# MLP units in features form: high and low parts of x side by side, 512 columns a product, in a fp32-by-parts transformer kernel

## The reference, cut to what matters

```
def squared_relu_mlp(hn, w_up, w_down):
    return jnp.square(jax.nn.relu(hn @ w_up)) @ w_down
...
hf = _rms_norm(x, norm_ffn_pre[l])
u = _dwconv_causal(hf @ w_up[l], ffn_dw[l]) + ffn_dw_b[l]      # 3 taps along the tokens
u_g, u_v = jnp.split(u, 2, axis=-1)
yff = (jax.nn.silu(u_g) * u_v) @ w_down[l]
```

## Time and profile before

| | |
|---|---|
| median of 3 runs | 1291.28 us (1290.41 to 1294.0) |
| profiled execution | 1293.13 us, of which the span of instructions is 1291.4 us |
| PE busy | 98% of the span, 9836 matmuls |
| DVE busy | 64%; ACT 52% |
| DMA | 210.89 MB, mean 163 GB/s |
| granted TensorE clock | 0.993 of full speed on average |
| MLP 0, first product to last up unit's ReLU | 229.8 to 399.3 us |
| MLP 1, the same | 528.9 to 698.3 us |
| FFN, first product to the end of the span | 1098.7 to 1291.4 us |

### The profile page before, as it was taken

One profiled execution on the slowest core, in us unless ns is written; L12 is line 12 of the kernel. 1 busy time (PEld: TensorE's weight loads), 2 busy tenths in 40 slices (PEclk: granted clock), 3 DMA queues, 4 the chain that ended last, 5 costly groups with the idle time before them and its releaser, 6 DMA issues.

```text
span 1291.4 us, 23651 instructions
## 1 busy us (share of the span) xinstructions
PE 1259.2 (98%) x9836; PEld 1181.3 (91%) x9836; DVE 832.1 (64%) x1136; ACT 667.3 (52%) x935; POOL 58.6 (5%) x101
## 2 busy tenths in 40 slices
PE   8999899999999999999999999999999998999998
PEld 7998898999998998899998999999999987999997
DVE  5984357655556565655555579998656566776665
ACT  5973646454445544544444554655454445655543
POOL 4001011000000000000000000010000010000000
PEclk9999999999999999999999999999999999999999
DMA  7660114656554644465655466344546533555551
GB/s 233 184 185 34 69 35 162 217 207 190 178 185 145 229 133 163 139 204 194 195 192 166 153 207 187 121 147 134 174 154 196 196 118 111 180 196 196 181 177 65
DMA packets 160345, 210.89 MB, mean 163 GB/s; under 512 B 5542, under 2 KB 143220, under 8 KB 160261
## 3 DMA queue, kind: packets, MB, share of 16 engines
q1 hardware_dynamic: 157315, 202.77, 48.7%
q0 software_dynamic: 1904, 6.85, 1.5%
q10 hardware_dynamic: 1042, 0.07, 0.1%
HBM read 208.62 MB, written 1.05 MB: 162 GB/s over the span
## 4 chain that ended last, share of the span: by engine, by line
PE 83%; DVE 8%; ACT 3%; issue 2%; DMA 2%; SPq 1%; POOL 0%; DVEq 0%; POOLq 0%; ACTq 0%
PE bank L365 25%; PE bank L368 25%; PE bank L369 25%; DVE wlo L301 2%; PE bank L1275 2%; PE bank L1255 2%; ACT whi L293 1%; DMA raw<-in_dn_w_in 1%; ACT common L611 1%; PE bank L1283 1%; SPq L3125 1%; PE bank L1811 1%; DVE common L2351 1%; PE bank L1938 1%; PE bank L1897 1%
## 5 line engine op out<-in xcount | busy, mean ns | idle before, releaser
L301 DVE TENSOR_TENSOR wlo<-raw,whi 128x2048 fp32r<-128x2048 f32 x190 | 434.8, 2291 | 239.5 <-ACT whi L293 239.3
L365 PE MATMUL bank<-xhi,whi 128*128 128x256 f32 x1808 | 519.8, 288 | 6.6 <-DVE xlo L688 6.2
L369 PE MATMUL bank<-xhi,wlo 128*128 128x256 f32 x1808 | 513.4, 284 | 0.0
L368 PE MATMUL bank<-xlo,whi 128*128 128x256 f32 x1808 | 513.3, 284 | 0.0
L293 ACT ACTIVATE whi<-raw 128x2048 fp32r<-128x2048 f32 x190 | 362.7, 1911 | 167.5 <-PE bank L365 108.4
L365 PEld LDWEIGHTS bank<-xhi,whi 128*128 128x128 f32 x1808 | 348.2, 193 | 12.0 <-issue 7.7
L368 PEld LDWEIGHTS bank<-xlo,whi 128*128 128x128 f32 x1808 | 348.3, 193 | 2.8 <-issue 1.2
L369 PEld LDWEIGHTS bank<-xhi,wlo 128*128 128x128 f32 x1808 | 348.2, 193 | 0.0
L365 PE MATMUL bank<-whi,hhi 128*128 128x512 f32 x392 | 153.4, 391 | 0.8 <-DVE hlo L2658 0.8
L368 PE MATMUL bank<-wlo,hhi 128*128 128x512 f32 x392 | 153.1, 391 | 0.0
L369 PE MATMUL bank<-whi,hlo 128*128 128x512 f32 x392 | 152.7, 389 | 0.0
(11 more groups left out here) (350 smaller groups left out, 1509.7 us busy)
## 6 DMA issues: line engine op xcount, KB each, us to landing
raw<-in_mlp_w_up SPq DMA_DIRECT2D x32, 1024.0 KB, 5.4
raw<-in_mlp_w_down SPq DMA_DIRECT2D x32, 1024.0 KB, 4.9
raw<-in_w_in SPq DMA_DIRECT2D x22, 1024.0 KB, 5.3
raw<-in_w_up SPq DMA_DIRECT2D x22, 1024.0 KB, 5.1
raw<-in_w_gate SPq DMA_DIRECT2D x16, 1024.0 KB, 5.5
raw<-in_dn_w_in SPq DMA_DIRECT2D x15, 1024.0 KB, 5.8
raw<-in_mb_w_in SPq DMA_DIRECT2D x12, 1024.0 KB, 5.1
raw<-in_w_down SPq DMA_DIRECT2D x11, 1024.0 KB, 4.9
```

The costliest lines, as they stand in the source:

```text
L301: nc.vector.tensor_tensor(wlo[:, s, :], raw[:, V % RAW, :], f32(whi[:, s, :]), ALU.subtract).then_inc(lo_ready, 1)
L365: ins = pe.matmul(o, shi, mhi, start=first, stop=False, skip_group_check=True)
L368: pe.matmul(o, shi, mlo, start=False, stop=False, skip_group_check=True)
L369: return pe.matmul(o, slo, mhi, start=False, stop=last, skip_group_check=True)
```

## The change

In the up units of the two MLPs and of the FFN, and nowhere else, `xhi` and `xlo` become two halves of one tensor `xparts`, and two matmuls per (f, k) take the place of three: the low weights against `xhi` (256 columns, into columns 0 to 255 of a bank) and the high weights against `xhi` and `xlo` side by side (512 columns, into the whole bank). f = 0 and f = 1 have a bank each. The two sums in a bank are then added: ACT copies columns 256 to 511 to SBUF (`copy_low`), DVE adds columns 0 to 255 to it (`add_low`) and gives the bank back. In the MLP, ReLU then works in place in SBUF. In the FFN, Identity and the taps read the sum from a new place `cin`, one for each half. In the first unit of a stage, the products of the low weights come first and wait only for `xhi`.

```
+        def wide_features(pe, U, uses, n=0, i=0, norm=None):
+            s = U % RING
+            pe.wait_ge(lo_ready, at_unit(U + 1, n, i))
+            wh, wl = wview(whi, s, KT), wview(wlo, s, KT)
+            def low_weights(f, k, start):
+                return pe.matmul(uses[f].ps[:, 0:T], wl[:, k, f * P:(f + 1) * P], xhi[:, k, :], start=start, stop=False,
+                                 skip_group_check=True)
+            def high_weights(f, k, stop):
+                return pe.matmul(wide_sums(uses[f]), wh[:, k, f * P:(f + 1) * P], xparts[:, :, k, :], start=False,
+                                 stop=stop, skip_group_check=True)
...
+                for f in range(2):
+                    if uses[f].n:
+                        pe.wait_ge(uses[f].freed, uses[f].at(i))
+                    for k in range(KT):
+                        ins = low_weights(f, k, k == 0)
+                        if f == 0 and k == 0:
+                            ins.then_inc(unit_begun, 1)
+                        ins = high_weights(f, k, k == KT - 1)
+                    ins.then_inc(uses[f].filled, 1)
+        def copy_low(act, dst, uses, copied, i=0, f=None):
+            for f in range(2) if f is None else [f]:
+                act.wait_ge(uses[f].filled, uses[f].at(i) + 1)
+                nc.scalar.activation(dst[:, f * T:(f + 1) * T], uses[f].ps[:, T:2 * T], ACT.Copy)\
+                    .then_inc(copied[f].sem, 1)
+        def add_low(dve, dst, uses, copied, i=0, f=None):
+            for f in range(2) if f is None else [f]:
+                part = dst[:, f * T:(f + 1) * T]
+                dve.wait_ge(copied[f].sem, copied[f].at(i))
+                nc.vector.tensor_tensor(part, uses[f].ps[:, 0:T], part, ALU.add).then_inc(uses[f].freed, 1)
...
             def act_a(act, U, p_, uses, hi_, re_, copied, n=0, i=0):
                 split_hi(act, U, n, i)
+                copy_low(act, hid_r[:, p_, :], uses, copied, i)
+                for use in uses:
+                    act.wait_ge(use.freed, use.at(i) + 1)
+                nc.scalar.activation(hid_r[:, p_, :], hid_r[:, p_, :], ACT.Relu).then_inc(re_.sem, 1)
...
             def act_half(act, b, half, i):
                 split_hi(act, b.us[half], b.n, i)
+                copy_low(act, src, b.uses[half], b.low[2 * half:2 * half + 2], i)
+                for use in b.uses[half]:
+                    act.wait_ge(use.freed, use.at(i) + 1)
...
             def dve_half(dve, b, half, i):
                 split_lo(dve, b.us[half], b.n, i)
+                add_low(dve, src, b.uses[half], b.low[2 * half:2 * half + 2], i)
                 dve.wait_ge(b.y1[half].sem, b.y1[half].at(i))
```

More of the change, by code:

```diff
@@ L169, in build @@
         wlo = sb("wlo", [P, RING, UNIT], F32R)
[L170 to L171 removed]
+        xparts = sb("xparts", [P, 2, KT, T], F32R)
+        xhi, xlo = xparts[:, 0], xparts[:, 1]
         hhi = sb("hhi", [P, 2, 2, T], F32R)
@@ L417, in gemm_features, with wide_sums @@
             ins.then_inc(use.filled, 1)
+        def wide_sums(use):
+            return use.ps[:, :].rearrange("p (x t) -> p x t", x=2)
+        def wide_features(pe, U, uses, n=0, i=0, norm=None):
[8 more added lines that the diff above has]
+                                 stop=stop, skip_group_check=True)
+            if norm:
+                for half in range(2):
+                    for q in (half, 2 + half):
+                        pe.wait_ge(norm.hi[q].sem, norm.hi[q].value)
+                    for f in range(2):
+                        if half == 0 and uses[f].n:
+                            pe.wait_ge(uses[f].freed, uses[f].n)
+                        for k in range(4 * half, 4 * half + 4):
+                            ins = low_weights(f, k, k == 0)
+                            if f == 0 and k == 0:
+                                ins.then_inc(unit_begun, 1)
+                    for q in (half, 2 + half):
+                        pe.wait_ge(norm.parts[q].freed, norm.parts[q].n + 1)
+                    for f in range(2):
+                        for k in range(4 * half, 4 * half + 4):
+                            ins = high_weights(f, k, k == KT - 1)
+                        if half:
+                            ins.then_inc(uses[f].filled, 1)
+            else:
+                for f in range(2):
+                    if uses[f].n:
+                        pe.wait_ge(uses[f].freed, uses[f].at(i))
+                    for k in range(KT):
+                        ins = low_weights(f, k, k == 0)
+                        if f == 0 and k == 0:
+                            ins.then_inc(unit_begun, 1)
+                        ins = high_weights(f, k, k == KT - 1)
+                    ins.then_inc(uses[f].filled, 1)
@@ L888, in mlp @@
             dl = [unit(rows(down, 256 * (NB - 2))), unit(rows(down, 256 * (NB - 1)))]
[L889 to L894, removed]
+            ua = [[G[2 * p_ + f].use() for f in range(2)] for p_ in range(2)]
@@ new lines, in mlp @@
+            hi_s, f_s, lo_s, re_s = (x.many(2) for x in (hid_sq, hid_f32, hid_lo, hid_relu))
+            cp_s = [low_sum.many(2) for p_ in range(2)]
+            ul = [[G[2 * p_ + f].loop(loop, 1)[0] for f in range(2)] for p_ in range(2)]
+            hi_l, f_l, lo_l, re_l = (x.loop(loop, 2) for x in (hid_sq, hid_f32, hid_lo, hid_relu))
+            low = low_sum.loop(loop, 4)
+            cp_l = [low[0:2], low[2:4]]
+            ut = [[G[2 * p_ + f].use() for f in range(2)] for p_ in range(2)]
@@ L2744, in conv_mlp @@
             prod = [common[:, 2048 + 512 * b_:2560 + 512 * b_] for b_ in range(2)]
+            cin = [common[:, 3072 + 512 * half:3584 + 512 * half] for half in range(2)]
             y1 = Signal(sem("ffn_first_tap"))
@@ L2815, in static_block @@
                 us = [unit(features(W, 256 * j)), unit(features(W, FF + 256 * j))]
-                marks = (y1.many(2), mid.many(2), sl.next(), pr.next(), hid_sq.next(), hid_lo.next())
-                uses = [G[2 * (j % 2) + k].use() for k in range(2)]
+                marks = (y1.many(2), mid.many(2), taps.many(2), low_sum.many(4), sl.next(), pr.next(), hid_sq.next(), hid_lo.next())
+                uses = [[G[2 * half + f].use() for f in range(2)] for half in range(2)]
                 b = Blk(j % 2, 2 * j, 0, us, marks, uses)
@@ L2905, in pe_block @@
                 for half in range(2):
-                    gemm_features(pe, b.us[half], b.uses[half], xhi, xlo, b.n, i, norm=None if half else norm)
+                    wide_features(pe, b.us[half], b.uses[half], b.n, i, norm=None if half else norm)
             def pe_f(pe):
```

112 lines of the change are left out of this document (55 added, 57 removed).

## The result

The changed kernel takes **1310.56 us** (median of 4 runs, 1309.7 to 1314.09), the kernel before 1292.64 us beside it (4 runs, 1290.41 to 1294.01): a ratio of 1.0147, 95% interval 1.0126 to 1.0167. It is slower, as predicted, but by 17.9 us and not 9.6, and 1310.56 lies outside the range of 1294 to 1309.

What follows compares the result with a forecast made beforehand. PE bounded all three stages before; changed, the DVE-ACT chain would bound the FFN. MLPs -6.9, FFN +14.5 and clock +2 gave +9.6 us: 1301 us against 1291.3, range 1294 to 1309.

Steps and rivals of the forecast that it cites:

- the ring: FFN: `add_low` behind `split_lo` closes a serial chain through DVE and ACT, 18.1 us a block against PE's 16.53.
- Rival A: FFN: PE stays the bound, since DVE's work fits by sum; -11.4 us, 1280 us; chance 0.08.
- Rival B: FFN: the DVE-ACT chain holds but is short, 17.0 to 17.3 us; 1289 to 1295 us; chance 0.11.
- Rival C: Up units: the fixed 13.3 ns per matmul is not saved, only the chain is left; 1308 us; chance 0.06.
- the parts of the ring: FFN block: first half 6.15 us, second half with block end 11.97 us.
- one fixed 13.3 ns goes: Up units: each (f, k) falls from 360 to 346.7 ns, a unit from 5.76 to 5.55 us; MLPs -6.8 us.
- the additions at the ends of the MLPs: MLP ends: copy and additions lengthen the last chain, +0.45 us at MLP 0 and +0.9 us at MLP 1.
- The 0.9 us at the end of MLP 1: End of MLP 1: copy 0.42 and additions 0.45 us more, passed on whole to the addition to `h`.
- The earlier starts of the three stages: First unit of each stage: PE starts on `xhi` without `xlo`, 0.7 us earlier each, -2.1 us in all.
- Terms of the FFN: FFN: 201.7 us against 187.1, +14.6, taken as +15.2; +14.5 after the 0.7 us earlier start.
- The first block: FFN: the first block takes 15.2 us, 5.97 + 9.2, with taps in place of a down unit's Silu and splits.
- The clock at the end: FFN end: after PE idles some 10 us, last products run at the lower clock level, +2 us (0 to 3.5).

Runs made afterwards that it cites:

- After: The changed kernel as made, measured and profiled against the kernel before; 1310.56 us, ratio 1.0147.
- Experiment 2: Changed kernel with the two MLPs put back to three matmuls per (f, k), the FFN left changed; 1313.88 us, ratio 1.0162.
- experiment 4: Changed kernel with DVE's two additions ahead of the split of the weights in the FFN; 1293.28 us, ratio 1.0008.
- 8: Changed kernel with one more 128x256 addition on DVE ahead of the additions of every FFN half but the last; 1318.4 us, ratio 1.0207.
- 9: The kernel of experiment 4 with one more 128x256 addition on DVE for every FFN half but the last; 1293.29 us, ratio 1.0018.
- experiment 10: The kernel of 7 with, for each f, the eight low-weight matmuls first and then the eight of 512 columns; 1285.07 us, ratio 0.9961.
- Experiment 3: Changed kernel with the high and low part of x for one k side by side in memory; 1309.88 us, ratio 1.0138.
- experiment 5: The kernel of Experiment 3 with operand and bank also written as one flat run of 512 columns; 1314.07 us, ratio 1.0157.
- 1: Changed kernel with the FFN put back to three matmuls per (f, k), the two MLPs left changed; 1289.48 us, ratio 0.9986.
- 6: The kernel of experiment 4 with unit 3's split behind the first unit's own ReLU, Square and `hlo` in each MLP; 1290.83 us, ratio 0.9995.
- 7: Changed kernel with the edits of experiment 4, experiment 5 and 6 together; 1290.17 us, ratio 0.9987.

## Why the prediction was right about the direction and wrong about the size

**Right: the ring.** The prediction said that `add_low` behind `split_lo` closes a chain through DVE and ACT that is longer than PE's work. After shows each sign of it: Identity released by `add_low`, 18.3 us a block, seven short waits of PE and one of 10.4 us. Experiment 2 puts the loss in the FFN, 4 removes it by the order alone, 8 and 9 show that an operation on the chain counts in one order and not in the other. Rival A (PE stays the bound) is out in after; experiments 4 and 10 made it true of the kernel, but not its 1280 us; the saving per matmul that it counts on came out smaller. Rival B (a ring of 17.0 to 17.3 us) is out. Rival C (13.3 ns not saved, 1308 us) came nearer to 1310.56 than the forecast of 1301, and about half of its premise holds, as the next step shows.

**Right: the parts of the ring.** The first half is 6.24 us (1267.38 to 1273.62) for 6.15, the second with the block's end 12.04 (to 1285.66) for 11.97. Together it is 18.28 for the 18.1 that the prediction went on with, 1.4 us over the eight blocks of the loop.

**The step that failed first: "one fixed 13.3 ns goes"** per (f, k), so an up unit of 5.55 us and MLPs of -6.8. Seven pairs in after take 305.82 to 308.29 = 2.47 us:

```profile
305.82 0.28 PE L431 MATMUL bank<-xparts,wlo 128*128 128x256 f32 x1
...
308.29 0.28 PE L431 MATMUL bank<-xparts,wlo 128*128 128x256 f32 x1
```

That is 353 ns and not 346.7: 7 ns go. The turn is 11.11 us, 0.11 less than in the earlier trace rows and not 0.23. The 120 and 227 ns of the earlier trace rows came from rows of one width each, and the prediction added them for a pair in which the widths alternate. 3.6 us are saved in the MLPs, 3.2 fewer than forecast. The Trainium skill (TensorE: Matmul & The Clock Gate, section Back-to-back issue gap) gives 2.5 ns per matmul for isolated ones; what was measured here, 7 ns, lies between this and 13.3. Experiments 3 and 5 rule out the two pieces and the pattern. In 10, eight wide ones in a row and eight narrow ones regain 4 of the 6 missing ns, so most belongs to alternating the widths. The other 2 are in the wide matmuls: in the group above, eight of them take 1.84 us (308.19 to 310.03), 230 ns each and not 227. Why either is so stays open.

**The step that was missing: the first unit of MLP 0.** The prediction priced the additions at the ends of the MLPs and held that in between "PE stays the bound". It had not looked at what stands ahead of the additions where a load comes late: the split that waits for it, 4.82 us already before the change. The 1.87 us wait above is followed by a lower clock (window, its length, PE, PEld, DVE, ACT, POOL, then the granted clock, DMA share, GB/s):

```profile
240.00:244.00 4.00, 2.13 (x8) 1.44 (x7) 2.34 (x3) 3.52 (x5) 0.00 (x0) 0.86 0.84 245
244.00:248.00 4.00, 4.00 (x15) 3.20 (x14) 3.20 (x5) 1.87 (x3) 0.00 (x0) 0.71 0.39 103
```

Products of 512 columns are 0.43 us apart there (243.50 to 243.92), the lower of the two levels. What the two windows lack to full speed is 0.14 x 4 + 0.29 x 4 = 1.7 us. With the wait it is 3.6 us of the profiled execution. Experiment 3's profile has a wait of 1.8 us at the same place and no lower clock, so the 1.7 us are not in every execution. Of the seven profiles with this wait (1.6 to 1.9 us: after and experiments 1, 3, 4, 5, 8 and 9), two have the lower clock behind it, after and experiment 5. That the additions' place behind the split makes the wait is borne out by experiments 6 and 7, where the split goes behind them and the longest such wait is 0.5 us.

Both together explain why the FFN starts only 0.6 us earlier (1098.08 against 1098.68 in the earlier trace rows) and not 7.6: 3.2 and 3.6 of the 7.0 us that are missing. The 0.9 us at the end of MLP 1 came as forecast: the last product starts at 696.32 and ReLU at 697.68, 1.36 us later, where it was 0.32 (697.41 to 697.73), and 0.11 of the difference is that the product is now the wider one. From ReLU to the addition to `h` it is 5.3 us in both. The earlier starts of the three stages, 0.7 us each in the forecast, came about as it said: PE's waits for `xlo` fall by 2.9 us (6.2 in the earlier trace rows, 3.3 in after), and the first products now wait 0.9 us in sum for something else.

**Terms of the FFN.** From the first product to ACT's release in the last tile it is 208.00 us (1098.08 to 1306.08) for 186.47: +21.5, where 14.6 to 15.2 and 2 for the clock were forecast.

```profile
1306.08 0.60 ACT L671 ACTIVATE common<-bank 128x512 f32<-128x512 f32 x1 [4.11 <-PE bank L371]
```

The 4.3 us more are several small ones. The first addition comes 6.66 us after the start and not 6.0 (+0.7): ACT had copied the bank at 1103.41, but DVE was in its splits up to 1104.74. The first block takes 16.64 us and not 15.2 (+1.4): its first half is 7.01 us instead of 5.97, and the split in it waits 1.04 us for `split_hi`, which waits for a load; the rest is 9.63 instead of 9.2, with an `ACT_TABLE_LOAD` of 1.28 us ahead of Silu for which the product waits 0.46 us. Both the load (1107.65) and the table load (1111.52) stand in the trace of before, and the prediction left them out.

```profile
1104.74 0.75 DVE L477 TENSOR_TENSOR common<-bank,common 128x256 f32<-128x256 f32 x2
...
1109.54 2.29 DVE L303 TENSOR_TENSOR wlo<-raw,whi 128x2048 fp32r<-128x2048 f32 x1 [1.04 <-ACT whi L295]
1111.75 0.75 DVE L477 TENSOR_TENSOR common<-bank,common 128x256 f32<-128x256 f32 x2
...
1121.38 0.74 DVE L477 TENSOR_TENSOR common<-bank,common 128x256 f32<-128x256 f32 x2
...
1295.32 0.99 DVE L2958 TENSOR_TENSOR hlo<-common,hhi 128x256 fp32r<-128x256 f32 x2
```

The nine blocks behind it take 164.28 us (1121.38 to 1285.66) and not 162.6 (+1.7, 1.4 of it the loop's). The last half's way to `hlo` is 10.65 us (to 1296.31) and not 9.7 (+0.9). That is 4.7 us, of which 0.6 was in the +15.2 already.

**The clock at the end** was priced about rightly. The last products begin at 1295.89, after the wait of 10.4 us, in the first of these windows:

```profile
1290.00:1298.00 8.00, 2.11 (x5) 1.76 (x6) 4.30 (x10) 2.55 (x7) 0.00 (x0) 0.55 0.00 0
1298.00:1302.00 4.00, 4.00 (x12) 3.12 (x12) 0.69 (x1) 1.38 (x4) 0.00 (x0) 0.62 0.00 0
```

The first twelve take 5.2 us (to 1301.09), where at the 227 ns of the earlier trace rows they would take 2.7: 2.5 us for a term of +2.

**The sum again:** -0.6 up to the FFN and +21.5 in it are +20.9 of the span's +21.0. Two small sums of the prediction do not come out, and neither matters: the terms of DVE's turn in an MLP make 8.3 us and not 8.5, and the second adding-up of the FFN, 14.6 and 0.8 more, would be 15.4 where 15.2 was taken. Of the gap to the forecast on this profile, 11.4 us, 7.0 are ahead of the FFN and 4.3 in it.

## What to carry to other kernels

When an evacuation from PSUM gets a new step on an engine that also has long work of its own, look first at what stands ahead of the new step in that engine's order: here the kernel with four additions a block, 1.5 us, is 18 us of 1293 slower than before with them behind a 2.2 us split, and 1 us, not to be told from none, with them ahead of it. PE's saving from fewer, wider matmuls should be read from pairs of the very widths that will follow each other, and where they alternate, group them. Before trusting that an engine keeps the pace, go through the first unit of each stage as well as the steady turn, since a load that comes late there holds everything queued behind it, and a wait that cost nothing before (4.82 us in MLP 0) can do so once the chain behind it is longer.

## What the runs showed of the hardware that was not expected

- A matmul of 256 columns and one of 512 in turn take 353 ns a pair, in rows of one width 120 + 227 = 347. In groups of eight it is 349 ns, of which the wide one takes 230. Neither the distance of the operand's two pieces nor a pattern of two levels is the reason.
- Waits of PE of up to 1.3 us once in each 18 us block left the granted clock at 1.00; the wait of 10.4 us was followed by 0.55 and 0.62, one of 1.87 us by 0.86 and 0.71 in one execution, and one of 1.8 us in experiment 3's by no lower clock. In experiment 10 the clock of 1260 to 1276 is 1.00 with a wait of 3.0 us in it, while in experiment 4 a wait of 2.8 us is followed by 0.74. The same length of wait was thus met with and without the lower level. The loop of the FFN in after:

```profile
1150.00:1290.00 140.00, 126.64 (x653) 105.83 (x651) 98.77 (x129) 73.46 (x100) 0.00 (x0) 1.00 0.48 159
```
